# Keys projected once for both key heads, mLSTM gates on four column tiles with a summing product, and first token transposes between the modulation pieces

## The reference, cut to what matters

```python
u = h * (1 + sc1) + sh1            # six modulation vectors per layer from silu(c) @ w_mod + b_mod
a_in, q, k, v, mq, mk, mv, mo, mg, bg = split_in(u @ w_in[l])
kh = axial_rope(k.reshape(B, S, N_KV_HEADS, HEAD_DIM), row_pos, col_pos)    # 2 key heads of 64
g_lat = mg.reshape(B, S, 2, 2, N_MLSTM_HEADS) + gate_b    # direction, type, head: 16 gate columns
```

## Time and profile before

| | us |
|---|---|
| median of three runs | 1807.72 |
| the profiled execution | 1811.84 |
| its span (first to last instruction) | 1810.0 |
| PE busy | 1657.3 (92%) |
| VectorE busy | 784.5 (43%) |
| ScalarE busy | 361.7 (20%) |
| GpSimd busy | 212.2 (12%) |
| mean granted TensorE clock | 0.969 |

### The profile page before, as it was taken

How to read it: one execution, slowest core, us unless ns; L and a number is a source line. 1 busy time by engine, 2 the same in 40 slices (tenths; PEclk the granted TensorE clock), 3 DMA queues, 4 the chain that set the end, 5 groups by cost and what they waited for, 6 DMA issues and landing times.

```text
span 1810.0 us, 31444 instructions
## 1 busy us (share of the span) xinstructions
PE 1657.3 (92%) x13046; PEld 998.2 (55%) x13046; DVE 784.5 (43%) x1580; ACT 361.7 (20%) x891; POOL 212.2 (12%) x225
## 2 busy tenths in 40 slices
PE   4999999899999999899999885999889997999984
PEld 1454475455444448654555444777578886555542
DVE  3069624366101112544235546592452114554555
ACT  1001025542000000312222112012631012111111
POOL 0300000000000000023333221000000000333321
PEclk8999999999999999999999997999999998999997
DMA  9722555630212323599569988432103465899994
GB/s 307 186 74 98 183 184 186 236 126 5 88 51 70 104 71 115 193 348 408 197 217 394 407 350 243 121 122 88 35 1 110 130 215 189 329 408 403 408 384 188
DMA packets 186815, 360.77 MB, mean 199 GB/s; under 512 B 22113, under 2 KB 106569, under 8 KB 186163
## 3 DMA queue, kind: packets, MB, share of 16 engines
q1 hardware_dynamic: 176800, 331.48, 51.3%
q0 software_dynamic: 8960, 22.87, 3.6%
q10 hardware_dynamic: 915, 4.42, 0.6%
HBM read 353.77 MB, written 10.35 MB: 201 GB/s over the span
## 4 chain that ended last, share of the span: by engine, by line
PE 66%; issue 13%; DVE 7%; POOL 5%; DMA 5%; ACT 3%; SPq 1%; DVEq 0%; POOLq 0%; ACTq 0%
PE psum L909 64%; DMA yab<-in_moe_w_gu 2%; POOL ys L859 2%; POOL qkT L842 2%; DMA uT<-in_moe_w_gu 1%; SPq L723 1%; PE psum L971 1%; DMA ring<-in_w_mod 1%; DVE hstat L1971 1%; DVE arena L2024 1%; PE psum L1346 0%; DVE ring L2255 0%; PE psum L1373 0%; ACT arena L1590 0%; POOL convT L818 0%
## 5 line engine op out<-in xcount | busy, mean ns | idle before, releaser
L909 PE MATMUL psum<-uT,ring 128*128 128x512 f32 (+1 forms) x1472 | 502.9, 502 | 0.0
L909 PEld LDWEIGHTS psum<-uT,ring 128*128 128x128 f32 x1472 | 279.9, 191 | 217.7 <-issue 200.8
L909 PE MATMUL psum<-ring,mo_tok 128*32 128x256 f32 x4992 | 310.5, 385 | 22.4 <-DVE ring L2255 20.7
L909 PEld LDWEIGHTS psum<-ring,mo_tok 128*32 128x32 f32 x4992 | 151.1, 110 | 138.6 <-DVE ring L2255 39.0
L909 PE MATMUL psum<-ring,v_tok 128*32 128x256 f32 x2496 | 152.3, 384 | 0.6 <-ACT v_tok L1698 0.4
L2255 DVE COPY ring<-yab 128x1024 f32<-128x1024 f32 x120 | 85.9, 752 | 123.7 <-PE psum L909 103.1
L1896 DVE SCALAR_TENSOR_TENSOR convT<-upad,cwT,convT 128x512 f32<-128x512 f32 (+1 forms) x240 | 132.4, 614 | 2.1
L2255 DVE COPY ring<-arena 128x1024 f32<-128x1024 f32 x120 | 81.0, 716 | 89.3 <-PE psum L909 66.0
L2089 DVE TENSOR_TENSOR arena<-psum,mqk 128x512 f32<-128x512 f32 (+1 forms) x16 | 8.9, 558 | 254.2 <-PE psum L909 254.2
L909 PE MATMUL psum<-ring,uT 128*128 128x256 f32 (+1 forms) x576 | 113.7, 357 | 0.0
L909 PEld LDWEIGHTS psum<-ring,v_tok 128*32 128x32 f32 x2496 | 75.8, 111 | 61.2 <-issue 16.0
(11 more groups left out here) (312 smaller groups left out, 1556.0 us busy)
## 6 DMA issues: line engine op xcount, KB each, us to landing
yab<-in_moe_w_gu SPq DMA_DIRECT2D x120, 512.0 KB
uT<-in_moe_w_gu SPq DMA_DIRECT2D x120, 512.0 KB
arena<-in_moe_w_dn SPq DMA_DIRECT2D x120, 512.0 KB
ring<-in_w_in SPq DMA_DIRECT2D x104, 512.0 KB, 4.7
ring<-in_w_mod SPq DMA_DIRECT2D x96, 512.0 KB, 6.1
ring<-in_w_out SPq DMA_DIRECT2D x16, 512.0 KB, 4.3
ring<-in_moe_w_gu SPq DMA_DIRECT2D x16, 512.0 KB, 8.2
ring<-in_w_a_out SPq DMA_DIRECT2D x8, 512.0 KB, 3.5
```

What stands on the lines that cost most here:

```text
L909: return nc.tensor.matmul(dst, lhsT, rhs, start=start, stop=stop)
```

## The change

Four things are changed:

- **Keys.** Slot "kk" holds the 128 key columns once, in two transfers instead of four. One `by_channel` call makes tile 4 with head 0 on partitions 0 to 63 and head 1 on 64 to 127. Tile 5 has no projection and no partner. After the rotary embedding VectorE makes the duplicates with three copies, and only then gives the last `rope_ready`.
- **Gates.** `wgate` shrinks to 32 columns for each of the 8 channel tiles, 16 of them real, loaded by one transfer instead of four. The eight matmuls run on four column tiles, channel tile k on tile k % 4. ScalarE copies the bank to `gate_sums`, and after the keys one 128x128 matmul with the constant `gate_select` adds the four partial sums and puts them in their rows (new tile "igs", which VectorE reads in place of "ig").
- **Start.** The latent transposes move from before piece 6 to before piece 1, the small rows from before piece 4 to before piece 2, the first context transposes from after the last piece to before piece 4.
- **Banks.** The list of PSUM tiles is one shorter in each layer.

```diff
-PREP_STEP = 4
-TOKENS_STEP = 6
+TOKENS_STEP, PREP_STEP, CONTEXT_STEP = 1, 2, 4
...
-        order += [("v", l), ("ig", l)]
-        order += [("qk", l, t) for t in (4, 5, 0, 1, 2, 3)]
-        order += [("perm", l, t) for t in range(6)]
+        order += [("v", l), ("ig", l), ("qk", l, 4), ("igs", l)]
+        order += [("qk", l, t) for t in range(4)]
+        order += [("perm", l, t) for t in range(5)]
...
+    gate_select = np.zeros((P, P), np.float32)
+    for j in range(16):
+        d, typ, h = j // 8, j // 4 % 2, j % 4
+        gate_select[j::32, 64 * typ + 32 * d + h] = 1.0
...
-        wgate = sb("wgate", [P, KD, P])
+        wgate = sb("wgate", [P, KD, 32])
+        gate_select = sb("gate_select", [P, P])
...
+            setup.append((gate_select[:, :], a["k_gates"]))
...
-                elif kind == "kk":
-
-                    copies = [(w8[:, :, (2 * g + r) * DH:(2 * g + r + 1) * DH],
-                               win[l][:, :, C_K + g * DH:C_K + (g + 1) * DH]) for r in range(2) for g in range(NKV)]
-                    pairs = copies[0:2]
-                    for dst, src in copies[2:4]:
-                        sp.dma_start(dst, src).then_inc(k_copy_loaded, 16)
+                elif kind in ("v", "kk"):
+                    c0 = C_V if kind == "v" else C_K
+                    pairs = [(w8[:, 4 * g:4 * g + 4, 0:P], win[l][:, 4 * g:4 * g + 4, c0:c0 + P]) for g in range(2)]
...
-                for typ in range(2):
-                    for d in range(2):
-                        c = C_MG + 8 * d + 4 * typ
-                        r = 64 * typ + 32 * d
-                        pool.dma_start(wgate[:, :, r:r + NH], win[l][:, :, c:c + NH]).then_inc(wgate_loaded, 16)
+                pool.dma_start(wgate[:, :, 0:16], win[l][:, :, C_MG:C_MG + 16]).then_inc(wgate_loaded, 16)
...
                         if s == TOKENS_STEP:
                             transposes(0, 0)
+                        if s == CONTEXT_STEP:
+                            transposes(0, 1, 0, 2)
                         modulation(x)
-                    transposes(0, 1, 0, 2)
                     modulation_columns(0)
...
-                by_channel(wgate, 0, T, "ig", l)
+                wait_bank(pe, "ig", l)
+                for k in range(KD):
+                    q = 32 * (k % 4)
+                    last = mm(bank("ig", l)[q:q + 32, :], wgate[:, k, :], uT[:, k, :], k < 4, k >= 4)
+                done(last, "ig", l)
                 wait_slot(pe, "kk", l)
-                pe.wait_ge(k_copy_loaded, 32 * (l + 1))
-                for g in range(NKV):
-                    by_channel(slot8(slot_of("kk", l)), g * P, T, "qk", l, 4 + g)
+                by_channel(slot8(slot_of("kk", l)), 0, T, "qk", l, 4)
+                wait_drained(pe, "ig", l)
+                wait_bank(pe, "igs", l)
+                done(mm(bank("igs", l)[:, :], gate_select[:, :], gate_sums), "igs", l)
...
-                for t in range(6):
+                for t in range(5):
...
+                wait_ready(act, "ig", l)
+                f(gate_sums, bank("ig", l)[:, :], ACT.Copy).then_inc(drained_of("ig", l), 1)
-                for t in (4, 5, 0, 1, 2, 3):
+                for t in (4, 0, 1, 2, 3):
...
-                wait_ready(dve, "ig", l)
-                v.tensor_scalar(grow[:, 7, :], bank("ig", l)[:, :], gate_bias[:, l:l + 1], None, ALU.add)\
-                    .then_inc(drained_of("ig", l), 1)
-                wait_drained(dve, "ig", l)
+                wait_ready(dve, "igs", l)
+                v.tensor_scalar(grow[:, 7, :], bank("igs", l)[:, :], gate_bias[:, l:l + 1], None, ALU.add)\
+                    .then_inc(drained_of("igs", l), 1)
+                wait_drained(dve, "igs", l)
...
-                dve.wait_ge(rope_ready, 6 * (l + 1))
+                dve.wait_ge(rope_ready, 6 * l + 5)
+                v.tensor_copy(qkT[64:128, 5, :], qkT[64:128, 4, :])
+                link(v.tensor_copy(qkT[0:64, 5, :], qkT[64:128, 4, :]))
+                v.tensor_copy(qkT[64:128, 4, :], qkT[0:64, 4, :]).then_inc(rope_ready, 1)
```

More of the change, by code:

```diff
@@ L289, in host_constants @@
         "k_perm": perm,
+        "k_gates": gate_select,
         "k_select": (np.arange(P)[:, None] % 32 == np.arange(32)[None, :]).astype(np.float32),
@@ L389, in build @@
         grow = arena
+        gate_sums = arena[:, 6, :]
         w_buf = arena
@@ L472, in build @@
         loaded = [sem(f"slot_loaded{s}") for s in range(NS)]
-        k_copy_loaded = sem("k_copy_loaded")
         c_rows_loaded, rows_loaded = sem("c_rows_loaded"), sem("small_rows_loaded")
@@ L599, in build @@
             used(("v", l), ("v", l))
-            used(("kk", l), ("qk", l, 5))
+            used(("kk", l), ("qk", l, 4))
             for c in range(2):
@@ L697, in load @@
                               win[l][:, :, C_A + g * D_CONV + j * P:C_A + g * D_CONV + (j + 1) * P]) for g in range(2)]
-                elif kind == "v":
-                    pairs = [(w8[:, 4 * g:4 * g + 4, 0:P], win[l][:, 4 * g:4 * g + 4, C_V:C_V + P]) for g in range(2)]
-                elif kind == "kk":
-                    copies = [(w8[:, :, (2 * g + r) * DH:(2 * g + r + 1) * DH],
-                               win[l][:, :, C_K + g * DH:C_K + (g + 1) * DH]) for r in range(2) for g in range(NKV)]
-                    pairs = copies[0:2]
-                    for dst, src in copies[2:4]:
-                        sp.dma_start(dst, src).then_inc(k_copy_loaded, 16)
+                elif kind in ("v", "kk"):
+                    c0 = C_V if kind == "v" else C_K
+                    pairs = [(w8[:, 4 * g:4 * g + 4, 0:P], win[l][:, 4 * g:4 * g + 4, c0:c0 + P]) for g in range(2)]
                 elif kind in ("q", "mqk", "mv", "mo"):
@@ L897, in _ @@
                 pool.wait_ge(x_loaded[h], 16)
-            pool.wait_ge(wgate_loaded, 64 * DEPTH)
+            pool.wait_ge(wgate_loaded, 16 * DEPTH)
             pool.wait_ge(setup_loaded, SETUP)
@@ L1021, in _ @@
                 pe.wait_ge(setup_loaded, SETUP)
-                pe.wait_ge(wgate_loaded, 64 * (l + 1))
-                by_channel(wgate, 0, T, "ig", l)
+                pe.wait_ge(wgate_loaded, 16 * (l + 1))
+                wait_bank(pe, "ig", l)
[3 more added lines that the diff above has]
+                done(last, "ig", l)
                 wait_slot(pe, "kk", l)
-                pe.wait_ge(k_copy_loaded, 32 * (l + 1))
-                for g in range(NKV):
-                    by_channel(slot8(slot_of("kk", l)), g * P, T, "qk", l, 4 + g)
+                by_channel(slot8(slot_of("kk", l)), 0, T, "qk", l, 4)
+                wait_drained(pe, "ig", l)
+                wait_bank(pe, "igs", l)
+                done(mm(bank("igs", l)[:, :], gate_select[:, :], gate_sums), "igs", l)
                 for c in range(2):
```

## The result

The changed kernel took 1788.49 us, median of 4 runs (1786.05 to 1789.88), against 1808.3 us for 4 runs of the kernel before (1807.6 to 1811.54). The ratio is 0.9877, with a 95% interval of 0.9858 to 0.9896; the plain quotient of the two medians is 0.9890 and lies inside it. The forecast was 1786.2 us in a range of 1780 to 1796. The two profiled executions stand at 1811.84 and 1789.14 us, 22.7 apart; the sum had said 1790.3 for the second.

What follows compares the result with a forecast made beforehand. PE's unbroken matmul stretches in the projections were taken to bound the kernel. Projections -22.6, start +1.2, columns +1.0 and scores -1.1 gave -21.5 us, from a median of 1807.7 to 1786.2 us, range 1780 to 1796.

Steps and rivals of the forecast that it cites:

- Keys -6.87, partner -0.46: Projections, each layer: one `by_channel` call less saves 6.87 us, one partner product less 0.46 us.
- Gates 6.87 to 2.05, sum +0.86: Projections, each layer: gates on four tiles fall from 6.87 to 2.05 us; the summing product adds 0.86 us.
- Copy hidden behind the keys: Before the summing product: ScalarE's bank copy, at most 0.75 us, is covered by 6.87 us of key product.
- VectorE's slack: VectorE loses 14.1 us against PE; layer 1's 27.86 us wait for the log takes this up, leaving 13.8.
- Start +1.2: Start: piece 7 and the columns product run at half clock, costing 1.2 us; bounds -0.5 and +1.2.
- Rival 1: Start: the clock is up when piece 7 arrives, so -0.5 us instead of +1.2, total 1784.5; chance 0.28.
- Columns of layer 0 +1.0: Layer 0, behind the last attention output: "cols" moves to bank 6 and waits 1.0 us; bounds 0 and 1.3.
- Scores of layer 1 -1.1: Layer 1, first scores: the 2.18 us bank wait goes, 1.1 us of it is gained; bounds 0 and -2.2.
- The total: Whole kernel: -21.5 us, giving 1790.3 us for the profiled execution and 1786.2 for the median; chance 0.55.
- Rival 2: Experts of layer 0: weight transfers end at the same time regardless, losing layer 0's 9.1 us, 1795.3; chance 0.09.
- Rival 3: Projections: the gate tiles do not overlap, 4.8 us more per layer, total 1795.8; chance 0.04.
- rival 4: Behind the start: the clock stays low, 1849 us if all work up to the gates ran low; chance 0.02.

Runs made afterwards that it cites:

- e5_gates_before: Against the changed kernel: gates back on the full array without a sum, single keys and new start kept; 1794.6 us, ratio 0.9905.
- e1_start_before: Against the changed kernel: small rows' transposes, their preparation and context transposes back in their old places; 1786.59 us, ratio 0.9855.
- e2_pad_both: Against the changed kernel: one small tile more in each layer, so every later tile has its old bank; 1788.45 us, ratio 0.9863.
- filled start: Against the changed kernel: unneeded identity transposes put in PE's gaps at the start; alone 1786.37 us, ratio 0.9856.
- e0_after: The changed kernel unaltered, measured again on another chip; 1787.36 us, ratio 0.9876.
- e10_after_again: The changed kernel unaltered, measured once more in the third group of runs; 1785.28 us, ratio 0.9862.

## Why the prediction was right, point by point

- **Keys -6.87, partner -0.46**: measured -6.87 and -0.43 in layer 0. For the keys the cost by rows of the same product held exactly.
- **Gates 6.87 to 2.05, sum +0.86**: the gates take 1.85 us from start to start, and the keys behind them 6.97 instead of 6.87, so that with both changes of shape the gates cost 1.95, nearer to the lower bound of 1.92 than to the 2.05 taken. The sum costs 0.86. Together that is 6.87 - 1.95 - 0.86 = 4.06 a layer; `e5_gates_before` gives 4.05, and 3.96 was forecast. Per layer the projections give -10.92 and the partner -0.43: 11.35 us where 11.29 was said. By the Trainium skill (TensorEngine Tiling (Array Packing), Theoretical Speedup) four tiles give up to four times the speed, which would be 1.72 for the gates (an estimate); the measured ratio is 6.87 / 1.85 = 3.7.
- **Copy hidden behind the keys**: yes, no idle time before the sum. ScalarE's copy takes 0.60 us, not the 0.75 taken from VectorE's, and without the keys as its cover PE stands for 0.76 us, and the stretch grows by 0.80 to 0.81.

```profile
111.06 0.60 ACT L1533 ACTIVATE arena<-psum 128x512 f32<-128x512 f32 x1 [1.29 <-PE psum L905]
```

- **VectorE's slack**: the wait for the log still holds 13.46 us in layer 1, forecast 13.8. The gate bias comes 4.55 us later, 1.74 of them from the start, so 2.81 where 2.8 was said (the row of before has it at 114.47; the forecast took 114.3):

```profile
119.02 0.75 DVE L1888 TENSOR_SCALAR arena<-psum,gate_bias 128x512 f32<-128x512 f32 x1 [5.44 <-PE psum L905]
...
232.58 0.68 DVE L1922 SCALAR_TENSOR_TENSOR arena<-arena 64x512 f32<-64x512 f32 x1 [18.98 <-ACT arena L1568]
...
1230.22 0.68 DVE L1922 SCALAR_TENSOR_TENSOR arena<-arena 64x512 f32<-64x512 f32 x1 [13.46 <-ACT arena L1568]
```

- **Start +1.2**: the mechanism was right (piece 7 and the columns product at half clock), the size +1.5 on the mean of eight executions, above the bound of +1.2. The start of the main stretch was forecast well: 1.1 us later (44.4 to 45.5), and 1.16 on the mean of the eight (44.22 to 45.38). The rest arises inside it, where the forecast has "PE restarts low in both kernels (0.76 on the mean between 44.4 and 48.0)": 63.59 us up to the gates on the mean of the eight, 63.11 before, with a clock between 44 and 48 of 0.50 to 0.67 against 0.73. But the old start also gave 63.80 and 0.64 (`e1_start_before`), so where the last tenths arise is not settled by two executions of it. Rival 1 (full clock at piece 7) did not occur in any unfilled execution of the new start, though its first half, the clock up behind piece 0, did.
- **Columns of layer 0 +1.0**: 1.02 us, as read off the bank list. What the step missed is the clock behind it: it said that the later units "move with it", and in 4 of 6 executions they also ran slower, for 3.3 us, a term that the forecast put at nothing. In the profiled execution the +1.0 became 1.02 + 3.55 = 4.6.
- **Scores of layer 1 -1.1**: 2.25 us were won before the first scores (-2.68, less 0.43 for the partner). From these to the second attention output it took 24.51 us before and 25.81 after, so 1.30 were given back: a net of 0.95, and 1.07 against `e2_pad_both`. Behind that the stage has low stretches in both: the product `convT,v_tok` behind the 2.40 us wait took 2.93 us before and 3.49 after (1.93 at full clock), and before, one at 1323.49 took 3.21 where it takes 1.89 after.
- **The total**: -19.8 between the medians, -22.7 between the profiled executions, -21.5 forecast. Measured again on two other chips the same change gave -23.0 and -25.8, so the forecast stands within the spread of the measurements, which is 6 us wide. Against the missed 3.55 stood low stretches of the kernel before: one at the start of the output stage (the granted clock between 440 and 500 was 0.97, after the change 1.00; -1.70), one behind 312 us that is 1.6 us longer than the same one after the change (inside the norms-to-columns line), and -1.89 at the experts, where the eleven experiments scatter from 338.69 to 341.57 us. So part of the closeness is luck: single terms of 2 to 4 us were missed on both sides.
- **Rivals 2, 3 and 4** did not occur. Rival 2 would have let the experts' stage grow by 9; it is no longer than before in any run, and the weight transfers moved along with PE. Rival 3 is excluded by the 1.85 us, rival 4 by the clock, 0.93 from 48 to 52 us and 0.99 on the mean from 48 to 100.

**What stays open:** whether the 1.02 us wait causes the low clock, or only coincides with it; and how much of the filled start's 3.05 us arrives at the end. A test for the first would fill the 1.36 us wait and leave the 1.02. For the second, the ratios lean that way (0.9856 against 0.9876 for the unfilled kernel of the same group) but overlap.

## What to carry to other kernels

In a stretch where PE is busy without a break, the time from start to start of the same operation priced an added or removed product to 0.1 us here; what could not be priced that well is each new idle time of PE, which cost its own length and, in some executions, several times that in clock. So compare the clock behind the same wait over several traces before a low stretch is put down to an edit. Look at the bank list when a tile is taken out: one tile less moved two waits here, one in and one out, far from the edit. And put work that needs another engine's copy behind something as long as the copy (here 6.87 us over 0.8).

## What the hardware showed that was not expected

- Modulation pieces of 1.94 us that come every 2.65 us kept the granted clock at 0.50 (34 to 37 us); with unneeded transposes in the gaps it was 1.00 with the same transfers. In `e0_after` the pieces 5 and 6 ran at full clock and piece 7 at half, so the fall has no fixed place.
- The granted clock of the table reads 1.00 at the first piece in all thirteen traces, while that piece takes 1.93 us, as at half clock; in the kernel before pieces 1 and 2 do too, under the same 1.00 (20 to 26 us). At the start of a kernel the durations are the better witness.
- Idle times of 1.36 and 1.02 us with 1.5 us of work between them were followed, 2 us later, by 6 to 7 us at half clock in 4 of 6 executions. The Trainium skill (TensorE: Matmul & The Clock Gate, A second HAM failure mode: psum-queue depth-cycling) tells of short idle times between groups of matmuls that make the clock swing between its two levels, which agrees with these rows; that it may happen or not in the same program at the same place, it does not say.
- Low stretches come back at the same places, behind waits of 2.4 to 2.9 us, in 7 to 13 of 13 executions, and lengthen the product behind the wait by 0.6 to 3.1 us. Whether one of them falls or not differs between executions of one program: `e10_after_again` has the one at the start of the output stage, `e0_after` has not (8.56 against 7.10 us). This is why the segments of a timeline told more here than the medians.
